# Two stacked two-layer transformer blocks on one core: operand addresses relative to the weight panels per sublayer, split down-projection matmuls, conditioning panels in the mixers' ends, selection rounds ahead of output tiles

## The reference, cut to what matters

```python
x = first_block(x, c, ...)      # 2 layers, each: FFN, mixer, FFN
return second_block(x, c_2, ...)  # 2 layers, each: mixer, FFN; rmsnorm at the end

# every sublayer, x is [256 tokens, 1024]:
mod   = silu(c) @ w_ada + b_ada                     # 9 (first) or 6 (second) vectors of 1024 per layer
h     = rms(x) * g * (1 + scale) + shift            # scale, shift, gate come from mod
x     = x + gate * sublayer(h)
ffn(h)   = (silu(h @ W_g) * (h @ W_u)) @ W_down     # 1024 -> 2816 -> 1024
mixer(h) = concat(normed branches of h @ w_in) @ w_out
# mixers of the first block: gated linear recurrence, stick-breaking and forgetting attention
# mixers of the second: pooling, chunk-band attention, attention over each row's top 64 keys,
#   latent attention; (256 tokens, 4 heads of 64 each)
```

## Time and profile before

| what | value |
|---|---|
| median of 3 runs | 1695.07 us (1691.84 to 1695.85) |
| profiled execution, its own time | 1691.13 us |
| its span, first to last instruction | 1689.3 us |
| PE matmul busy | 1621.6 us, 96% of the span, 12346 records |
| DVE busy | 1333.8 us, 79% |
| ACT busy | 912.1 us, 54% |
| mean granted TensorE clock | 0.990 |

### The profile page before, as it was taken

One profiled execution on the slowest core, in us unless ns is written; L12 is line 12 of the kernel. 1 busy time (PEld: TensorE's weight loads), 2 busy tenths in 40 slices (PEclk: granted clock), 3 DMA queues, 4 the chain that ended last, 5 costly groups with the idle time before them and its releaser, 6 DMA issues.

```text
span 1689.3 us, 30111 instructions
## 1 busy us (share of the span) xinstructions
PE 1621.6 (96%) x12346; PEld 1552.1 (92%) x12346; DVE 1333.8 (79%) x2113; ACT 912.1 (54%) x1567; POOL 85.0 (5%) x124
## 2 busy tenths in 40 slices
PE   2999999999999999999999999989999998999998
PEld 2999898999989999899899989989999898899997
DVE  6788899588889888887788888857888888485653
ACT  5455457664445545468654545656544466564553
POOL 4000000010000000000120001001000010010000
PEclk8999999999999999999999999999999999899999
DMA  9788775257878788753378878322788762145561
GB/s 355 301 318 325 272 280 197 100 190 305 325 264 312 271 325 319 297 222 144 107 251 317 318 280 325 126 75 101 295 318 327 296 237 101 55 171 199 225 250 50
DMA packets 57161, 403.10 MB, mean 239 GB/s; under 512 B 6606, under 2 KB 6866, under 8 KB 9280
## 3 DMA queue, kind: packets, MB, share of 16 engines
q1 hardware_dynamic: 55424, 396.01, 62.1%
q0 software_dynamic: 1600, 5.18, 1.0%
HBM read 400.10 MB, written 1.05 MB: 237 GB/s over the span
## 4 chain that ended last, share of the span: by engine, by line
PE 77%; DVE 13%; ACT 5%; DMA 3%; issue 1%; SPq 0%; DVEq 0%; ACTq 0%
PE PS L516 76%; DVE WL L1617 4%; DVE ring L1644 2%; ACT WH L1155 2%; DMA ring<-in_down 1%; DVE X L1620 1%; DVE SCR L1617 1%; DVE SCR L1620 1%; DVE HL L1620 1%; DMA SCR<-in_x 1%; ACT SCR L1441 1%; DVE SCR L1614 1%; DVE SMALL L2001 1%; DMA ring<-in_win 0%; ACT HH L1168 0%
## 5 line engine op out<-in xcount | busy, mean ns | idle before, releaser
L1617 DVE TENSOR_TENSOR WL<-ring,WH 128x1024 fp32r<-128x1024 f32 (+1 forms) x508 | 599.8, 1215 | 178.1 <-ACT WH L1155 177.2
L516 PE MATMUL PS<-HH,WH 128*128 128x256 f32 (+1 forms) x2640 | 650.5, 285 | 12.1 <-ACT WH L1155 9.5
L516 PE MATMUL PS<-HL,WH 128*128 128x256 f32 (+1 forms) x2640 | 639.2, 283 | 0.0
L1155 ACT ACTIVATE WH<-ring 128x1024 fp32r<-128x1024 f32 (+1 forms) x508 | 509.4, 1048 | 85.5 <-DMA ring<-in_down 47.8
L516 PEld LDWEIGHTS PS<-HH,WH 128*128 128x128 f32 x2640 | 495.9, 189 | 17.8 <-ACT WH L1155 9.7
L516 PEld LDWEIGHTS PS<-HL,WH 128*128 128x128 f32 x2640 | 494.5, 189 | 0.6
L516 PE MATMUL PS<-HH,WL 128*128 128x256 f32 (+1 forms) x2640 | 377.3, 280 | 3.1 <-DVE WL L1617 3.0
L516 PE MATMUL PS<-AHL,WH 128*128 128x512 f32 (+1 forms) x1188 | 373.5, 371 | 0.0
L516 PEld LDWEIGHTS PS<-HH,WL 128*128 128x128 f32 x2640 | 340.3, 189 | 4.2 <-DVE WL L1617 4.2
L1644 DVE CUSTOM_DVE_ANT_0 ring<-ring,CB,VC 128x1024 f32<-128x1024 f32 x240 | 316.3, 1339 | 9.4 <-DMA ring<-in_ada 9.4
L516 PE MATMUL PS<-AHL,WL 128*128 128x256 f32 x1056 | 297.4, 282 | 4.0 <-DVE WL L1617 3.9
(11 more groups left out here) (212 smaller groups left out, 1319.2 us busy)
## 6 DMA issues: line engine op xcount, KB each, us to landing
ring<-in_up SPq DMA_DIRECT2D x88, 1024.0 KB, 5.4
ring<-in_ada SPq DMA_DIRECT2D x72, 1024.0 KB, 7.0
ring<-in_ffn SPq DMA_DIRECT2D x66, 1024.0 KB, 4.9
ring<-in_mod SPq DMA_DIRECT2D x48, 1024.0 KB, 7.1
ring<-in_down SPq DMA_DIRECT2D x44, 1024.0 KB, 6.3
ring<-in_win SPq DMA_DIRECT2D x32, 1024.0 KB, 7.1
ring<-in_wout SPq DMA_DIRECT2D x16, 1024.0 KB, 4.8
ring<-in_winv SPq DMA_DIRECT2D x4, 1024.0 KB, 4.8
```

The costliest lines, as they stand in the source:

```text
L516: return e.matmul(out, lhsT, rhs, start=start, stop=stop, skip_group_check=skip)
L1155: e.activation(half_of(i)[0], slot_of(("unit", u))[:, w * (i % 2):w * (i % 2) + w], ACT.Copy).then_inc(s_hi, 1)
L1617: return e.tensor_tensor(out, a, b, op)
```

## The change

It does five things.

1. HH, HL, AH and AL get one view per sublayer, with rows whose length is a multiple of 256 bytes, at an offset from the table `AT_256`: the distance from the weights (modulo 256 bytes) is the same for all chunks and all four buffers. It is 192 in sublayers 0, 1, 4, 6 and 8, and 64, 128, 96, 160 and 224 in the FFNs 2, 3, 5, 7 and 9. YH and YL stay at 192.
2. AH and AL lie apart, so the 512-column matmul becomes two of 256 columns. `residual` is one operation.
3. `ADA_N` takes conditioning panels from the FFNs (22, 20, 21, 22, 21, 4 become 21, 19, 19, 17, 20, 4) to the mixers (2, 0, 0, 0 become 3, 2, 4, 3). In mixers they load at ticks 9 to 12, and DVE works them off one half at a time (`share`) among the out-projection's steps, where `gains(n + 1)` now stands too.
4. In mixer 2, DVE runs the last three selection rounds, `selected` and `pooled` ahead of the output tiles and of `lo(u0 + 10)`, PE and ACT move steps beside them.
5. `CB` holds one vector. The second is loaded once the last panel of the first block is used, and activated in sublayer 5.

```diff
-ADA_N = (22, 2, 20, 21, 0, 22, 0, 21, 0, 4)
+ADA_N = (21, 3, 19, 19, 2, 17, 4, 20, 3, 4)
-ADA_AT = {"mix1": (3, 5, 8), "mix2": (1, 2, 3)}
+AT_256 = (192, 192, 64, 128, 192, 96, 192, 160, 192, 224)
+ADA_AT = (9, 10, 11, 12)
...
-        HH = sb("HH", [128, KD, S + 2], F32R)
-        HL = sb("HL", [128, KD, S + 2], F32R)
+        HHL = []
+        for part in ("HH", "HL"):
+            part_at = nc.sbuf_base
+            sb("room_" + part, [128, KD * 320 + 64])
+            HHL.append([nc.alloc_sbuf_tensor_at(f"{part}{n}", [128, KD, 320], F32R, offset=part_at + AT_256[n]) for n in range(NSUB)])
+        HH, HL = HHL
...
-        AHL = nc.alloc_sbuf_tensor_at("AHL", [128, NF, 2, S], F32R, offset=scr_at)
-        AH, AL = AHL[:, :, 0, :], AHL[:, :, 1, :]
+        AH, AL = ([nc.alloc_sbuf_tensor_at(f"{part}{n}", [128, NF, S], F32R, offset=at + (64 + AT_256[n]) % 256) for n in range(NSUB)]
+                  for part, at in (("AH", scr_at), ("AL", scr_at + 4 * NF * S)))
...
-                    if c < KD - 1:
-                        both = PS[:, banks[c % len(banks)], :]
-                        mm(both, wh[:, g, :], AHL[:, k, :, :].rearrange("p a s -> p (a s)"), start=k == 0, stop=k == kt - 1, skip=True)
-                    else:
-                        mm(out, wh[:, g, :], AH[:, k, :], start=k == 0, stop=False)
-                        mm(out, wh[:, g, :], AL[:, k, :], start=False, stop=False)
+                    mm(out, wh[:, g, :], xh(k), start=k == 0, stop=False)
+                    mm(out, wh[:, g, :], xl(k), start=False, stop=False)
...
-                if c < KD - 1:
-                    step(stt(X[:, c, :], PS[:, b, 256:512], MOD[:, 24 * n + 16 + c:24 * n + 17 + c], X[:, c, :], ALU.mult, ALU.add))
-                stt(X[:, c, :], PS[:, b, 0:256], MOD[:, 24 * n + 16 + c:24 * n + 17 + c], X[:, c, :], ALU.mult,
+                stt(X[:, c, :], PS[:, banks[c % 6], 0:256], MOD[:, 24 * n + 16 + c:24 * n + 17 + c], X[:, c, :], ALU.mult,
...
+            def share(n, q):
+                if q < 2 * ADA_N[n]:
+                    ada_half(FIRST_ADA + sum(ADA_N[:n]) + q // 2, q % 2)
...
                 lo(u0 + 12)
+                share(n, 0)
                 partial(n, 2)
                 stick_tile(0)
                 stick_tile(1)
+                share(n, 1)
                 partial(n, 3)
                 diagonal(n, o0 + 2)
...
                 attended2(a0 + 1, o0 + 2)
-                largest(1, (5,))
+                largest(1, (5, 6, 7))
+                selected(1)
+                pooled(1, o0 + 3)
                 tile_rest(n, o0)
                 diagonal(n, o0 + 2)
-                largest(1, (6, 7))
-                selected(1)
-                lo(u0 + 10)
-                pooled(1, o0 + 3)
+                attended2(a0 + 2, o0 + 4)
+                lo_half(2 * u0 + 20)
                 tile_rest(n, o0 + 1)
                 diagonal(n, o0 + 3)
-                attended2(a0 + 2, o0 + 4)
+                maxima2(a0 + 3, 1)
+                lo_half(2 * u0 + 21)
...
+                    if c == 2:
+                        share(n, 7)
```

More of the change, by code:

```diff
@@ L83, in ada_halves @@
     else:
-        at = [q for q in halves if ADA_AT[SUBS[n][0]][q // 2] == t]
+        at = [q for q in halves if ADA_AT[q // 2] == t]
     return [(first + q // 2, q % 2) for q in at]
@@ L524, in cols @@
                         e.wait_ge(s_hh, 8 * n + k + 1)
-                    mm(out, wh[:, k, :], HH[:, k, 0:S], start=k == 0, stop=False)
+                    mm(out, wh[:, k, :], HH[n][:, k, 0:S], start=k == 0, stop=False)
                     if not first:
-                        mm(out, wh[:, k, :], HL[:, k, 0:S], start=False, stop=False)
+                        mm(out, wh[:, k, :], HL[n][:, k, 0:S], start=False, stop=False)
                 e.wait_ge(s_lo, i + 1)
                 for k in range(KD):
-                    last = mm(out, wl[:, k, :], HH[:, k, 0:S], start=False, stop=k == KD - 1 and not first)
+                    last = mm(out, wl[:, k, :], HH[n][:, k, 0:S], start=False, stop=k == KD - 1 and not first)
                 if first:
@@ L605, in tokens @@
                         for k in range(4):
-                            last = mm(out, HH[:, 4 * i + k, q], wl[:, k, :], start=False, stop=i == 1 and k == 3, skip=True)
+                            last = mm(out, HH[n][:, 4 * i + k, q], wl[:, k, :], start=False, stop=i == 1 and k == 3, skip=True)
                     last.then_inc(s_half, 1)
@@ L1212, in rounded @@
                     e.wait_ge(s_glu, NF * j + f + 1)
-                    e.activation(AH[:, f, :], G6[:, 3 + f % 3, :], ACT.Copy).then_inc(s_ah, 1)
+                    e.activation(AH[n][:, f, :], G6[:, 3 + f % 3, :], ACT.Copy).then_inc(s_ah, 1)
                 if n > 0:
@@ L1233, in ffn @@
                     if n == 0 and f == 16:
-                        e.wait_ge(s_cload, 32)
-                        e.activation(CB[:, 1, :], CB[:, 1, :], ACT.Silu).then_inc(s_cb, 1)
                         e.wait_ge(s_const_rest, 16)
@@ L1242, in ffn @@
                     e.activation(G6[:, f % 3, :], PS[:, up_bank(f), 0:256], ACT.Silu).then_inc(s_silu, 1)
+                    if n == 5 and f == 2:
+                        e.wait_ge(s_cload, 32)
+                        e.activation(CB[:, :], CB[:, :], ACT.Silu).then_inc(s_cb, 1)
                 hi_half(2 * (UNIT0[n] + NF + 1) + 1)
@@ L1551, in _ @@
             e.wait_ge(s_cload, 16)
-            e.activation(CB[:, 0, :], CB[:, 0, :], ACT.Silu).then_inc(s_cb, 1)
+            e.activation(CB[:, :], CB[:, :], ACT.Silu).then_inc(s_cb, 1)
             lnexp()
@@ L1578, in _ @@
                 e.activation(SQ[:, c, :], xr, ACT.Identity, bias=shift, scale=gain).then_inc(s_xn, 1)
-                e.activation(HH[:, c, 0:S], xr, ACT.Identity, bias=shift, scale=gain).then_inc(s_hh, 1)
+                e.activation(HH[0][:, c, 0:S], xr, ACT.Identity, bias=shift, scale=gain).then_inc(s_hh, 1)
                 if c == 5:
@@ L1894, in mixer1 @@
                 stick_softplus(0)
-                ada(n, 8)
                 lo(u0 + 10)
@@ L1920, in mixer1 @@
                 tile_rest(n, o0 + 2)
+                share(n, 3)
                 partial(n, 6)
                 tile_rest(n, o0 + 3)
+                share(n, 4)
                 partial(n, 7)
+                share(n, 5)
+                gains(n + 1)
                 lo(u0 + 13)
@@ L2111, in mixer2 @@
                 partial(n, 2)
+                share(n, 2)
                 tile_rest(n, o0 + 4)
@@ L2124, in mixer2 @@
                 tile_rest(n, o0 + 7)
+                share(n, 5)
                 partial(n, 7)
+                gains(n + 1)
+                share(n, 6)
                 lo(u0 + 13)
```

98 lines of the change are left out of this document (48 added, 50 removed).

## The result

The changed kernel takes **1679.4 us** in the median of 4 executions (1675.2 to 1682.1), the kernel before 1693.5 beside it (1691.0 to 1695.9): a ratio of 0.9915, interval 0.9887 to 0.9943. It is faster by 14 us, not by the 43 forecast, and inside the range only in its upper part.

What follows compares the result with a forecast made beforehand. The prediction took the kernel to be bound by how fast a PE busy 96% issues matmuls. Its terms summed as 1691.1 - 35.5 - 3 - 9 + 8.5 - 1 = 1651.1 us, called 1652; range 1632 to 1686.

Steps and rivals of the forecast that it cites:

- Term 1: Distances and split matmul in FFNs and mixers: two thirds at 113.3 ns, one third at 117.7; 35.5 us saved.
- signs of being wrong: Forecast wrong if the up parts' spacing stays at 118 ns, or if one new distance stands above 119.
- The split: FFN down parts: the 924 extra matmuls cost nothing; at 117.7 ns three take 353 ns, exactly the present pair.
- Term 2: FFN down parts: one residual operation instead of two shortens PE's waits for WL; 3 us saved, bounds 0 and 3.9.
- Term 3: Selection in each mixer 2: DVE work moves behind the pooled tile; 4.5 us saved each, 9 in sum, bounds 0 and 9.4.
- Term 4: Conditioning in the mixers' ends: 8.5 us added, bounds 0 and 32.2; mixer 1's front gives back 1 us.
- The side remark: FFNs: 14 panels fewer cost and save nothing, DVE being hidden behind PE; uncovered, 28 x 1.34 = 37 us.
- Term 5: CB's second vector, load and activation: some 10 us to spare before the first panel, so zero; if late, a few us.
- No gain from distances: Rival: all matmul streams settle at 117.7 ns, giving 1683 us; chance 0.14.
- slower: Rival: five FFNs with new distances settle at 123 ns, giving about 1721 us; decides from a mean of 119.3; chance 0.06.
- DVE became no bound: Rival: in the up parts DVE can't follow in half the ticks, half their gain is lost; about 1668 us; chance 0.07.
- Distance is nothing: Rival: up parts stay as they are, the split costs nothing, shares cost two or three us more; 1689 us; chance 0.06.

## Why the prediction was wrong

**What bounds the kernel** was read rightly: PE is busy 96% before and after, and the reading that the spacing depends on the two addresses and on the phase in which a stream starts, and that a constant 192 settles on 113.3 or 117.7 ns, stood in every run.

**Term 1 is the step that failed.** "I take two thirds at the floor and one third at 117.7." The range for a constant distance that no row showed went from the floor to 124 ns, and I took the value inside it from c = 7, whose distance is 192. The four unseen distances that the table gives to FFNs 3, 5, 7 and 9 hold 118.7, 120.0, 117.3 and 118.3 ns, where the drifting one had 118.0, 119.7, 118.0 and 119.1: two of them are worse than before, and none comes near the floor. By their spacing the up parts gave 10.5 us where I had 32.9, and 4.8 of the 10.5 are the draw of FFN 2, which has 64: in two later runs with the same table it stood at 117.8. One of the prediction's own signs of being wrong, a new distance above 119, came with the 120.0 of 96. The number for 192 was nearly right where 192 stands: FFN 0's up part gained 4.3 of my 5.0 us. The bounds did hold the outcome (the mean of the five new ones is 117.5 ns), the rows weighed for a middle did not bear on it. That all FFNs should have got 192 is what the run with it shows: 1661.5 us.

**The split** cost nothing, as the prediction had it. **Term 2**, 3 us, was right in mechanism: the waits for WL went from 1.8 to 0.2 us in FFN 0's down part, and split and single residual together give 5 us when nothing else is changed. The waits hang on DVE's load and on PE's pace too: without shares, with 22 panels in FFN 0 instead of 21 and its stream at the floor, they were 1.3 us again and the down part took 62.2 us.

**Term 3** was half of what it is: 9 us against 17 measured alone. The wait was priced rightly, 4.7 each. What I left out is the half clock behind it. The windows that the sum rests on lay in the steady parts, where the clock is 1.00. A table of 100 us windows of the same trace had 0.97 for 1100 to 1200 and 0.95 for 1400 to 1500, where these two stretches lie, and the prediction makes nothing of it.

**Term 4** was right in size, 7.5 us net against 9 from the run without shares, but partly by luck. The wait for the diagonal grew by 1.9 us in each mixer 1, close to the 2.2 forecast. By the profiles, taking the shares out makes the ends 7.5 us and the starts of FFNs 2 and 7 8.6 us shorter, and the fronts 4.3 and FFN 0's down part 1.9 us longer. The starts, and the half-clock stretches of 3.4 to 6.8 us behind the waits, the sum did not have. The side remark was wrong as well: the FFNs lose 10 panels (110 to 100), not 14, so 20 halves or 27 us and not 28 and 37; it was priced at nothing and moved no sum.

**Term 5**, zero: no wait of DVE for the vector shows.

**The sum.** By ratios the parts are: selection -17, split and residual -5, shares +10 (the changed kernel against the one without them), together -12 of the measured -14. The distances as dealt out are left with some 2 us, inside the uncertainty of these ratios (0.3%, 5 us); with FFN 2 at its upper value the spacing alone would give 5.7. Against the forecast, terms 1 and 2 gave 7 us instead of 38.5, term 3 gave 8 us more, and term 4 cost 1.5 to 2.5 us more: 31.5 - 8 + 2 is 25.5 us, and the forecast was 27 us too low.

**The rivals.** "No gain from distances", 1683 us with a chance of 0.14, was nearest in time and in the mean spacing, though it had all streams at 117.7. The "slower" rival was the right kind of mechanism, a distance that holds a bad value, with the point of decision at 119.3 ns in the mean of five; the mean was 117.5. DVE became no bound in the changed kernel (though PE had waited for it in an up part before, 1.0 us for WL at the start of FFN 0, where the prediction says never), but PE's waits for WL come back in FFN 5's down part once its stream runs at the floor. "Distance is nothing" falls: one table entry moves 1500 equal matmuls between 113.3 and 120.0 ns at a granted clock of 1.00. The rule of the Trainium skill ("TensorE: Matmul & The Clock Gate", Part 2) that the streamed operand and the weight load have independent read ports would leave the spacing alone; the measurement decides here, though what in the chip ties the two addresses together no run shows.

## What to carry over

A value read at one address, size or phase belongs to that one: where an edit sets six streams to five values that no row shows, give each its own line in the sum, with a value in the middle of what the trace's uneven spacings span, not the best steady value seen elsewhere. Read the granted clock behind every long wait of TensorE, not only in the steady parts: a wait there may cost nearly twice its length (here 8.3 us for one of 4.7), and so may a wait that an edit adds. And where one kernel's executions spread by over 1%, look whether a long stream has two steady values; here a single short matmul chose between them.
